# Starting the projections from the scaled activations: tile-by-tile turning, another order of the first loads, and the shift added as a bias

## The reference

```python
ada = silu(cvec) @ w_ada + b_ada                  # one vector c for the context, one for the latents
shift1, scale1, gate1, shift2, scale2, gate2 = split(ada, 6)
h = rmsnorm(x, norm1_w) * (1.0 + scale1) + shift1  # (640, 1024)
proj = h @ w_in                                    # 1024 -> 1024 + 1536 + 32 + 1024
z, xBC, dt_raw, v = split(proj)
xBC = silu(depthwise_conv(xBC))                    # 4 taps along the tokens
...                                                # scans, pooling of v, output product, experts
```

## Time and profile before

| | |
|---|---|
| runs of the kernel before | 939.12, 939.94, 941.73 us (median 939.94) |
| the profiled execution's own time | 939.72 us |
| its span, from the first to the last instruction | 937.9 us |
| PE busy | 841.9 us, 90% of the span |
| DVE, ACT, POOL busy | 383.1, 185.2, 210.9 us |
| mean granted clock of TensorE | 0.962 |
| traffic with the memory | 199.17 MB, mean 212 GB/s |

### The profile page before, as it was taken

How to read it: one execution, slowest core, us unless ns; L and a number is a source line. 1 busy time by engine, 2 the same in 40 slices (tenths; PEclk the granted TensorE clock), 3 DMA queues, 4 the chain that set the end, 5 groups by cost and what they waited for, 6 DMA issues and landing times.

```text
span 937.9 us, 18426 instructions
## 1 busy us (share of the span) xinstructions
PE 841.9 (90%) x7846; PEld 470.1 (50%) x7846; DVE 383.1 (41%) x773; ACT 185.2 (20%) x490; POOL 210.9 (22%) x255
## 2 busy tenths in 40 slices
PE   1899999999899999989999992999998999999940
PEld 1656655555554555554444441555554555555520
DVE  2430002643566588782322457522222222222228
ACT  5121000211232544431000012111111111111113
POOL 0169999700131433320000000000000000000022
PEclk9999999999999999999999996799999999999985
DMA  9942755781320000287000004599999899998327
GB/s 361 419 174 92 273 214 232 243 324 45 135 56 1 1 0 1 90 343 267 1 22 23 23 22 168 190 401 420 389 395 420 335 399 387 410 407 318 133 84 276
DMA packets 42520, 199.17 MB, mean 212 GB/s; under 512 B 7439, under 2 KB 16967, under 8 KB 25415
## 3 DMA queue, kind: packets, MB, share of 16 engines
q1 hardware_dynamic: 22032, 162.84, 43.6%
q0 software_dynamic: 6224, 22.55, 6.9%
q10 hardware_dynamic: 14183, 12.61, 4.3%
HBM read 175.80 MB, written 22.18 MB: 211 GB/s over the span
## 4 chain that ended last, share of the span: by engine, by line
PE 60%; DVE 7%; DMA 3%; issue 1%; ACT 1%; ACTq 0%; POOL 0%; POOLq 0%; DVEq 0%
PE bank L941 19%; PE bank L808 14%; PE bank L954 9%; PE bank L675 7%; DMA slot_out<-yT 2%; PE bank L931 2%; PE bank L773 1%; PE bank L946 1%; DVE ex L1662 1%; PE bank L713 1%; PE bank L783 1%; DVE xs L2041 1%; PE bank L760 1%; PE bank L757 1%; DMA ex<-slot_out,ri 1%
## 5 line engine op out<-in xcount | busy, mean ns | idle before, releaser
L599 PE MATMUL bank<-hT,ring 128*128 128x512 f32 (+1 forms) x640 | 178.6, 438 | 1.5 <-DVE hT L1551 1.5
L599 PEld LDWEIGHTS bank<-hT,ring 128*128 128x128 f32 x640 | 96.0, 193 | 72.1 <-issue 69.6
L1962 DVE TENSOR_TENSOR bcT<-bcT,bank 128x128 f32<-128x128 f32 x51 | 14.6, 287 | 167.7 <-ACT bcT L1288 167.7
L941 PE MATMUL bank<-ex,yT 128*32 128x256 f32 x1216 | 75.9, 393 | 1.2 <-ACT yT L1298 1.2
L941 PE MATMUL bank<-ring,yT 128*32 128x256 f32 x1248 | 76.6, 387 | 0.0
L675 PE MATMUL bank<-ring,hT 128*128 128x512 f32 x160 | 73.4, 593 | 0.1
L808 PE MATMUL bank<-ring,yT 128*128 128x512 f32 x160 | 70.9, 593 | 0.8 <-DVE yT L1723 0.8
L1477 POOL DMA_INDIRECT yT<-h_dram,token_of x16 | 15.5, 969 | 237.5 <-PE bank L931 220.3
L1469 POOL TENSOR_TENSOR ex<-ex,dts 128x512 f32<-128x512 f32 x40 | 45.2, 1132 | 83.2 <-ACT ex L1196 83.2
L1196 ACT ACTIVATE ex<-bank,dts 128x128 f32<-128x128 f32 x160 | 45.4, 369 | 49.1 <-PE bank L760 49.0
L941 PEld LDWEIGHTS bank<-ex,yT 128*32 128x32 f32 x1216 | 37.7, 113 | 28.1 <-issue 3.5
(11 more groups left out here) (312 smaller groups left out, 1175.6 us busy)
## 6 DMA issues: line engine op xcount, KB each, us to landing
ex<-w_exp SPq DMA_DIRECT2D x36, 1024.0 KB, 16.4
ring<-w_exp SPq DMA_DIRECT2D x36, 1024.0 KB, 15.0
ring<-w_ring SPq DMA_DIRECT2D x13, 2048.0 KB, 12.0
yT<-w_late SPq DMA_DIRECT2D x16, 1024.0 KB, 6.5
hT<-w_exp SPq DMA_DIRECT2D x12, 1024.0 KB, 14.8
uT<-w_exp SPq DMA_DIRECT2D x12, 1024.0 KB, 17.2
slot_out<-ex POOLq DMA_DIRECT2D x13, 512.0 KB, 17.1
ex<-x SPq DMA_DIRECT2D x5, 512.0 KB, 7.2
```

The source lines that it names most:

```text
L599: mm = pe.matmul(o, w[:, k, (f % 4) * P:(f % 4 + 1) * P], hT[:, k, lo:hi], start=(k == 0), stop=(k == KT - 1))
L941: mm = pe.matmul(psb[v % 2][g * TU:(g + 1) * TU, 0:256], xgT[b][:, k, u * TU:(u + 1) * TU], w[:, kk, g, :], start=(k == 0), stop=(k == KT ...
L1962: tt(ab[v % 2], sg[v % 2], psb[v % 2][:, P:2 * P], ALU.mult).then_inc(s_ac, 1)
```

## The change

- **Loads.** The two chunks of scale1 come first, then the first chunk of `w_in` (feature tiles 0 to 3), all three into the ring; the two chunks of shift1 follow, one into the spare buffer, one into ring buffer 0 when it is free. The second chunk of `w_in` takes ring buffer 1; the third (feature tiles 8 to 11) stands behind two more halves of `w_ada`, which wait for `ada_late(0)`.
- **x.** Each tile is squared, its root taken, scaled, transposed (eight transposes of one tile, four each into two banks) and copied (ACT one bank, DVE the other) before the next but one.
- **h.** DVE multiplies `hT` by `modA` alone; feature tiles 0 to 2 are projected from that (`UNSHIFTED = 3`). Between tiles 1 and 2, PE makes the two ada products of shift1; within tile 2 their rows are turned; after tile 2, `project_shift` multiplies the weights of tiles 0 to 2 by `modB` (24 matmuls of two columns). ACT adds these numbers as a bias when it copies tiles 0 to 2. After tile 2, DVE adds `modB` to `hT`, and from tile 3 on all is as before.
- **Later steps.** The products for dt and the decays follow tiles 3, 4 and 5 in place of 0, 1 and 2; the later parts of ada stand in the middle of tiles 6 to 13 in place of after 3 to 10; `turn_conv` starts after tile 13 in place of 11 and ends with three in place of two among the products of B and C; five of the eight later rows of ada are copied between DVE's convolutions. Some semaphores are joined into one; this moves no instruction.

```diff
-ADA_AT = (3, 4, 5, 6, 7, 8, 9, 10)
+ADA_AT = (6, 7, 8, 9, 10, 11, 12, 13)
+UNSHIFTED = 3
...
+        def shift_part(f):
+            return psb[1][:, 3 * P + 2 * f:3 * P + 2 * f + 2]
+        def x_banks(j):
+            return (psb[6], psb[7]) if j % 2 == 0 else (psb[4], psb[5])
...
             load_ada(1)
             sp.dma_start(invb, inv.to_broadcast([P, INV_ALL])).then_inc(s_inv, 16)
+            for u in range(2, 4):
+                load_ada(u)
             load_ring(5)
-            for u in range(2, 8):
+            for u in range(4, 8):
                 load_ada(u)
...
             for j in range(NJ):
                 pe.wait_ge(s_xn, j + 1)
-            for k in range(KT):
-                if k >= 2:
-                    pe.wait_ge(s_hl, k - 1)
-                    pe.wait_ge(s_hc, k - 1)
-                q = 6 - 2 * (k % 2)
-                for j in range(NJ):
-                    o = psb[q + 1][:, 0:P] if j == 0 else psb[q][:, (j - 1) * P:j * P]
-                    mm = pe.transpose(o, xt[:, j, k * P:(k + 1) * P], ident)
+                if j >= 2:
+                    pe.wait_ge(s_hl, j - 1)
+                    pe.wait_ge(s_hc, j - 1)
+                for k in range(KT):
+                    mm = pe.transpose(x_banks(j)[k // 4][:, (k % 4) * P:(k % 4 + 1) * P],
+                                      xt[:, j, k * P:(k + 1) * P], ident)
                 mm.then_inc(s_xtr, 1)
-            for n in range(4):
+            def turn_ada(n0):
+                pe.wait_ge(s_arc, n0 + 2)
+                for n in range(n0, n0 + 2):
+                    mm = pe.transpose(psb[0][:, n * P:(n + 1) * P], arow[:, n * P:(n + 1) * P], ident)
+                mm.then_inc(s_ar, 1)
+            for n in range(2):
                 ada_first(n)
-            pe.wait_ge(s_arc, 4)
-            for n in range(4):
-                mm = pe.transpose(psb[0][:, n * P:(n + 1) * P], arow[:, n * P:(n + 1) * P], ident)
-            mm.then_inc(s_ar, 1)
+            turn_ada(0)
...
+            def project_shift(f):
+                if f == 0:
+                    pe.wait_ge(s_mod, 2)
+                w = ring[:, 2, :].rearrange("p (k c) -> p k c", k=KT)
+                for k in range(KT):
+                    mm = pe.matmul(shift_part(f), w[:, k, f * P:(f + 1) * P], modB[:, 2 * k:2 * k + 2],
+                                   start=(k == 0), stop=(k == KT - 1))
+                return mm
...
-                if f:
-                    for k in range(KT):
-                        mm = project_features(f, k)
-                    mm.then_inc(s_fm, 1)
+                for k in range(KT):
+                    if f == UNSHIFTED - 1 and k == KT // 2:
+                        turn_ada(2)
+                    if f in ADA_AT and k == KT // 2:
+                        ada_late(ADA_AT.index(f))
+                    mm = project_features(f, k)
+                mm.then_inc(s_fm, 1)
+                if f == UNSHIFTED - 2:
+                    ada_first(2)
+                    ada_first(3)
+                if f == UNSHIFTED - 1:
+                    for i in range(UNSHIFTED):
+                        mm = project_shift(i)
+                    mm.then_inc(s_sft, 1)
...
-                if f == 11:
+                if f == 13:
                     turn_conv(0)
-                elif 13 <= f:
-                    turn_conv(f - 12)
+                elif 14 <= f:
+                    turn_conv(f - 13)
...
+                    if i == 4:
+                        turn_conv(7)
...
-                if f < KT:
+                if f < UNSHIFTED:
+                    c = stat[:, 5 + 2 * f:7 + 2 * f]
+                    if f == 0:
+                        act.wait_ge(s_sft, 1)
+                        act.activation(stat[:, 5:5 + 2 * UNSHIFTED], psb[1][:, 3 * P:3 * P + 2 * UNSHIFTED],
+                                       ACT.Copy).then_inc(s_sfc, 1)
+                        act.wait_ge(s_sfc, 1)
+                    act.activation(uT[:, f, 0:CTX], psb[q + 1][:, 0:CTX], ACT.Identity, bias=c[:, 0:1])
+                    act.activation(uT[:, f, CTX:TOK], psb[q][:, :], ACT.Identity, bias=c[:, 1:2]).then_inc(s_vr, 1)
+                elif f < KT:
...
-                    ins = ts(hT[:, k, lo:hi], hT[:, k, lo:hi], modA[:, i:i + 1], modB[:, i:i + 1], ALU.mult, ALU.add)
-                ins.then_inc(s_hs, 1)
+            modulate(modA, ALU.mult)
+            for n in range(2, 4):
+                ada_row(n)
+            dve.wait_ge(s_ar, 2)
+            tt(kc(modB[:, :]), sums[:, 1, :, 0:2], kc(vec[:, V_ADA:V_ADA + 16]), ALU.add).then_inc(s_mod, 1)
+            dve.wait_ge(s_mod, 2)
+            dve.wait_ge(s_hs, KT)
+            dve.wait_ge(s_fm, UNSHIFTED)
+            modulate(modB, ALU.add)
...
-    parts = [chunk(w_ada, 512 * i) for i in range(4)]
-    parts += [chunk(w_in, c0) for c0 in (v0, v0 + 512, x0 + D, x0, x0 + 512, 0, 512)]
+    parts = [chunk(w_ada, 1024), chunk(w_ada, 1536), chunk(w_in, v0), chunk(w_ada, 0), chunk(w_ada, 512)]
+    parts += [chunk(w_in, c0) for c0 in (v0 + 512, x0 + D, x0, x0 + 512, 0, 512)]
```

More of the change, by code:

```diff
@@ L548, in ada_first @@
                     pe.wait_ge(s_silc, 1)
[L549 removed]
+                if n < 2:
                     pe.wait_ge(s_ring[n], 16)
+                if n == 2:
+                    pe.wait_ge(s_mod, 1)
+                if n == 3:
+                    pe.wait_ge(s_ring[0], 32)
                 for k in range(KT):
[L552 removed]
+                    if n == 2 and k % 4 == 0:
                         pe.wait_ge(s_adaw[k // 4], 16)
[L554 to L555 removed]
+                    w = adaw[k // 4][:, k % 4, :] if n == 2 else ring[:, n % 3, k * 512:(k + 1) * 512]
+                    mm = ada_product(psb[n % 2], w, k, k == 0, k == KT - 1)
                 mm.then_inc(s_used, 1)
@@ L1071, in _, with square_x, copy_x @@
             act.activation(nega[:, :], row[:, R_ALOG:R_ALOG + 32], ACT.Exp).then_inc(s_soft, 1)
-            for j in range(NJ):
+            def square_x(j):
                 act.wait_ge(s_x[j], 16)
                 act.activation(junk_x, xt[:, j, :], ACT.Square, accum_out=stat[:, j:j + 1]).then_inc(s_ss, 1)
-                act.wait_ge(s_ss, j + 1)
-            act.wait_ge(s_eps, 1)
-            rms(0, NJ)
-            for k in range(KT):
-                act.wait_ge(s_xtr, k + 1)
-                act.activation(hT[:, k, CTX:TOK], psb[6 - 2 * (k % 2)][:, :], ACT.Copy).then_inc(s_hl, 1)
+                act.wait_ge(s_ss, 2 * j + 1)
+                if j == NJ - 1:
+                    rms(j)
+                else:
+                    r = stat[:, j:j + 1]
+                    act.activation(r, r, ACT.Sqrt, scale=1.0 / D, bias=eps_col[:, :]).then_inc(s_ss, 1)
+            def copy_x(j):
+                act.wait_ge(s_xtr, j + 1)
+                act.activation(hT[:, 0:4, j * P:(j + 1) * P], x_banks(j)[0][:, :].rearrange("p (k t) -> p k t", k=4),
+                               ACT.Copy).then_inc(s_hl, 1)
+            act.wait_ge(s_eps, 1)
+            for j in range(NJ):
+                square_x(j)
+                if j >= 1:
+                    copy_x(j - 1)
+            copy_x(NJ - 1)
             def silu_conv(f):
@@ L1523, in ada_row, with scale_x, copy_x @@
                 dve.wait_ge(s_used, n + 1)
-                dve.tensor_copy(arow[:, n * P:(n + 1) * P], psb[n][:, 0:P]).then_inc(s_arc, 1)
-            dve.wait_ge(s_rs, 1)
-            step(dve.reciprocal(stat[:, 0:NJ], stat[:, 0:NJ]))
-            for j in range(NJ):
-                ts(xt[:, j, :], xt[:, j, :], stat[:, j:j + 1], None, ALU.mult).then_inc(s_xn, 1)
-            for k in range(KT):
-                dve.wait_ge(s_xtr, k + 1)
-                dve.tensor_copy(hT[:, k, 0:CTX], psb[7 - 2 * (k % 2)][:, 0:CTX]).then_inc(s_hc, 1)
-            for n in range(4):
+                dve.tensor_copy(arow[:, n * P:(n + 1) * P], psb[n % 2][:, 0:P]).then_inc(s_arc, 1)
+            def scale_x(j):
+                if j == NJ - 1:
+                    dve.wait_ge(s_rs, 1)
+                else:
+                    dve.wait_ge(s_ss, 2 * j + 2)
+                r = stat[:, j:j + 1]
+                step(dve.reciprocal(r, r))
+                ts(xt[:, j, :], xt[:, j, :], r, None, ALU.mult).then_inc(s_xn, 1)
+            def copy_x(j):
+                dve.wait_ge(s_xtr, j + 1)
+                dve.tensor_copy(hT[:, 4:8, j * P:(j + 1) * P],
+                                x_banks(j)[1][:, :].rearrange("p (k t) -> p k t", k=4)).then_inc(s_hc, 1)
+            for j in range(NJ):
+                scale_x(j)
+                if j >= 1:
+                    copy_x(j - 1)
+            copy_x(NJ - 1)
+            for n in range(2):
                 ada_row(n)
@@ L1594, in _ @@
             tt(dtdec, dt_, dec, ALU.mult).then_inc(s_dtd, 1)
-            for q in range(NQ):
+            for q in range(NQ - 5):
                 ada_rows_out(q)
```

78 lines of the change are left out of this document (39 added, 39 removed).

## The result

The changed kernel takes 950.2 us (median of four runs, 945.2 to 952.7) against 939.9 before: ratio 1.0103, 95% interval 1.0080 to 1.0126. That is slower, as forecast, but by 10 us in place of 4.5, and above the range. The profiled execution is the fastest of the four, 945.2 us with a span of 943.4.

A forecast was written before the change was run, and what follows sets the result against it. PE was taken as the bound from the first feature tile on, waiting for data before it. Terms summed to +1.5 us, plus 3.0 for the clock: +4.5 on 939.72, forecast median 944.4 us, range 938.5 to 948.8.

The forecast's parts named there:

- start of tile 0: First feature tile on PE: to start at 28.6 us in place of 37.99, a gain of 9.4 us.
- two ada chunks, turned rows: On PE after tile 0 starts: ada products of two chunks cost +3.7 us, their two turned rows +0.3.
- shift products at full clock: Between tiles 2 and 3 on PE: 48 passes at 0.118 us each, +5.7 us, hidden by nothing.
- ACT's copy ahead of tile 3: Tile 3 takes tile 0's banks and waits for ACT to copy tile 0: +1.2 us, 0.9 to 1.5.
- stall at the second turned tile: PE's 1.83 us wait there, from ACT's stores of ada rows, goes: -1.8 us; 0 if it returns.
- one more round in the tail: After tile 19, three turned tiles each wait for DVE's copy of the one before: +1.8 us.
- clock behind the shift products: Granted clock falls in the narrow stretch ahead of tile 3 or behind it: +3.0 us, between 0 and 4.5.
- dt and the decays keep their distance to each other: Products for dt and the decays, moved behind later feature tiles: listed among edits at no cost.
- the clock did not hold: Rival: clock holds through the shift products, or their fall replaces the one behind L653; +1.5, 941.4 us, chance 0.24.
- the loads did not hide: Rival: weight loads hide in the shift products, 1.5 us instead of 5.7; 937.2 us or less, chance 0.10.
- The late start: Rival: TensorE stays at its lower level up to tile 0, which starts at 32.5; 948.3 us, chance 0.14.
- The rule that the prediction weighed against the 0.118 us: Trainium skill: some 25 ns per narrow matmul, next weights loading meanwhile; the 48 passes would take 1.2 us.

The follow-up runs named there:

- wide_shift: Changed kernel with the 24 shift products given a moving operand of 128 columns in place of 2; 946.3 us, ratio 1.0072.
- tail_back: Changed kernel with the second turned tile made within tile 14, leaving two behind tile 19; 946.8 us, ratio 1.0083.
- before_pool: Kernel before with POOL's windows begun behind DVE's softplus chain and the pooling weights loaded ahead of the last window tile; 935.7 us, ratio 0.9948.
- pool_waits: Changed kernel with POOL's windows begun only when DVE has finished the softplus chain; 946.7 us, ratio 1.0081.
- dt_later: Changed kernel with the products of the decays moved from behind tile 5 into tile 6, behind its second k; 942.0 us, ratio 1.0023.
- best_b: best_a plus 24 thrown-away transposes on PE ahead of those of x; 935.9 us, ratio 0.9956.
- shift_in_tile2: Changed kernel with shift1's ada products behind tile 0 and the 24 shift products between the matmuls of tile 2; 947.2 us, ratio 1.0088.
- row_shift: Changed kernel with shift1's ada products behind tile 0 and shift products within tile 2, padded modB (32 columns) stationary; 945.6 us, ratio 1.0058.
- best_a: Changed kernel joining row_shift, tail_back and pool_waits, with the pooling weights loaded ahead of the last window tile; 935.9 us, ratio 0.9960.

## Why the prediction was wrong, point by point

| step | predicted | profiled | |
|---|---|---|---|
| start of tile 0 | -9.4 | -8.5 | 0.9 late |
| two ada chunks, turned rows | +4.0 | +3.8 | held |
| shift products at full clock | +5.7 | +5.5 | held (wide_shift) |
| ACT's copy ahead of tile 3 | +1.2 | +1.3 | held |
| stall at the second turned tile | -1.8 | -1.8 | held |
| one more round in the tail | +1.8 | +1.8 | held (tail_back) |
| clock behind the shift products | +3.0 | +4.1 | too small |
| wait at the decays | 0 | +1.4 | missed |
| clock behind that wait | 0 | +1.6 | missed |
| sum at the pooled products | +4.5 | +9.1 | rows add up to 9.2 |

**The step that failed** is "dt and the decays keep their distance to each other", put among the edits at no cost. The distance is one feature tile, 9 us, and the chain that has to fit into it already overran it in the kernel before by the 0.53 us in front of L653: it was as long as its cover.

```profile
68.36 2.47 PE L653 MATMUL bank<-dts,cst 128*128 128x16 f32 x20 [0.53 <-DVE dts L1576]
```

Its length is set by where POOL's instructions fall, 9.2 us before, 10.5 to 11.7 in the changed variants. The excess is a wait, 1.89 less 0.53, and the fall behind it costs 10.35 - 6.93 = 3.4 us where the kernel before paid 1.8 (13.40 us from L653 to L542, against 11.63 in before_pool). Together 3.0 of the 4.6 us that were missed; pool_waits, which touches nothing but POOL, removed the wait and the fall at that place.

**The clock term** had the right mechanism and the wrong size: the fall began inside the stretch, as at the end of the bounds given (4.4), and I took the middle. My reading of L653 was also too simple. Its 2.8 us of narrow products sank nothing where no wait stood ahead of them (pool_waits, before_pool), and 1.3 us of waiting behind wide products sank nothing either (wide_shift, ahead of tile 3). With a wait ahead of the narrow products the clock fell in every profile of this place, be the wait 0.17 us (dt_later) or 3.07 (wide_shift, where it fell ahead of the products: its mean was 0.62 from 99 to 100 us, and they began at 99.67). The shift products, twice as long, sank it with no wait ahead of them. What decides in between is not shown. The fall in the kernel before slowed the tile behind it, so its wait of 0.53 us came with 2.3 us in all.

**The start** was late by 0.9 on the side of the activations: the ada products ended at 27.36 in place of 26.6, and 2.1 us passed from there to tile 0 in place of 2.0. The weights had landed by then, at 28.4 (22.1 us after their issue), not at 27.5. I had the half pace of the first transposes as a reason for a late start. best_b is without it: its ada products end at 24.3, and tile 0 then waits for the weights until 28.15. So in the changed kernel's profile curing the half pace was worth 1.1 us at most, 29.5 less 28.4.

**The range** ended at 948.8, and +9.1 us alone, with everything behind 260 us as before, gives 949.0. It also left no room for that stretch to move: what lies behind the pooled products varied by 6 us between profiles, and tiles 0 and 1 by 1.7.

**The rivals:** the clock did not hold, and the loads did not hide. The late start had its half pace in a part of it, and tile 0 never began later than 31.5 us. The rule that the prediction weighed against the 0.118 us does not hold here: the passes took 0.115 us even with 128 columns (wide_shift), and 0.11 between wide matmuls (shift_in_tile2).

## What to carry to other kernels

Before calling a moved chain free, measure how much its cover exceeds it; a chain that already leaves half a microsecond of wait is not covered, and beside a busy POOL its length is not its own. A product with few columns and 128 columns of weights was paid as a wide one here and cost the clock as well; with the narrow side as the stationary operand the same 48 passes took 1.95 us in place of 7.23. When a repaired variant wins, put each repair into the original alone: here POOL's wait, with one load moved ahead, was the gain.

## What was not expected of the hardware

- A POOL that works on buffers of its own slowed DVE by a factor of two: 16 additions of the shift took 9.54 us beside it and 4.83 without (row_shift, best_a). One operation on 128x160 elements took 1.58 us beside it and 0.24 without (the changed kernel, pool_waits). Three operations of POOL's own, on 128x512 elements, took 1.51 to 1.53 us beside those additions and 1.26 for a later tile (row_shift).
- Tile 0 ran at half clock at its start in some executions (0.50 from 30 to 32 us in best_a) and not in others, behind the same gap of 1.29 us (the changed kernel's profile: 1.00).
